# Inverse levels of a recurrent head on half the columns

## The reference

```python
def step(S, inp):
    r_t, w_t, k_t, v_t, a_t, b_t = inp
    Sa = jnp.einsum('bhij,bhj->bhi', S, a_t)
    S = S * w_t[:, :, None, :] + Sa[..., None] * b_t[:, :, None, :] + v_t[..., None] * k_t[:, :, None, :]
    y = jnp.einsum('bhij,bhj->bhi', S, r_t)
    return S, y
...
a = -kk ; b = kk * a_gate        # kk is k, normalised
```

## Time and profile before

| | us |
|---|---|
| median of 3 runs | 897.65 (894.34 to 900.71) |
| the profiled execution | 895.88 |
| its span | 894.1 |
| TensorE matmuls busy | 812.1 (91%) |
| TensorE weight loads busy | 510.3 (57%) |
| Vector engine busy | 457.0 (51%) |
| ScalarE busy | 248.7 (28%) |

### The profile page before, as it was taken

The page is one execution under the profiler, slowest core; times in us unless marked ns, Lnnn a source line. Parts: engine busy times, 40 slices in busy tenths (PEclk is TensorE's granted clock), DMA queues, the critical chain, the costliest instruction groups (busy, mean ns, idle before and its releaser), DMA issues.

```text
span 894.1 us, 16251 instructions
## 1 busy us (share of the span) xinstructions
PE 812.1 (91%) x6152; PEld 510.3 (57%) x6152; DVE 457.0 (51%) x1065; ACT 248.7 (28%) x584; POOL 64.8 (7%) x72
## 2 busy tenths in 40 slices
PE   3999999999999999999999989979899988888780
PEld 3566666666666666666666655456555544445440
DVE  1376687686686786886875936143221111111114
ACT  4123342351441432433423523220111111111112
POOL 1000000000000000000000000000322222222110
PEclk9999999999999999999999999975999999999995
DMA  9252060060250140320600512993999999999955
GB/s 221 78 134 73 25 167 15 25 170 8 58 144 23 45 134 23 105 73 23 166 12 23 165 30 60 375 413 119 344 386 387 385 396 391 392 392 388 399 203 180
DMA packets 114225, 159.85 MB, mean 179 GB/s; under 512 B 27470, under 2 KB 91528, under 8 KB 105974
## 3 DMA queue, kind: packets, MB, share of 16 engines
q1 hardware_dynamic: 98180, 149.14, 48.6%
q0 software_dynamic: 5136, 6.04, 2.5%
q10 hardware_dynamic: 10867, 4.09, 1.9%
HBM read 155.99 MB, written 13.64 MB: 190 GB/s over the span
## 4 chain that ended last, share of the span: by engine, by line
PE 70%; DMA 10%; DVE 8%; SPq 7%; issue 3%; ACT 1%; ACTq 1%; DVEq 0%; POOLq 0%
PE bank L627 17%; PE bank L1008 7%; SPq L457 5%; PE bank L633 4%; PE bank L914 4%; PE bank L795 4%; PE bank L1015 3%; PE bank L858 3%; DMA scratch<-in_exp_up 3%; DMA wall<-in_exp_up 3%; PE bank L738 3%; DMA vecs<-in_exp_up 2%; PE bank L649 2%; PE bank L745 2%; DVE vecs L1465 2%
## 5 line engine op out<-in xcount | busy, mean ns | idle before, releaser
L627 PE MATMUL bank<-xnT,wall 128*128 128x320 f32 x656 | 195.3, 442 | 1.8 <-DVE wkv L1571 1.8
L627 PEld LDWEIGHTS bank<-xnT,wall 128*128 128x128 f32 x656 | 119.0, 190 | 51.5 <-DVE wkv L1571 5.4
L1813 DVE SCALAR_TENSOR_TENSOR vecs<-vecs,bank 128x128 f32<-128x128 f32 x32 | 9.2, 287 | 144.7 <-ACT vecs L1360 144.7
L1008 PE MATMUL bank<-vecs,scratch 128*64 128x256 f32 x448 | 56.5, 409 | 9.1 <-DMA vecs<-in_exp_up 8.2
L1008 PE MATMUL bank<-scratch 128*64 128x256 f32 x384 | 45.8, 393 | 11.8 <-DMA scratch<-in_exp_up 10.6
L1809 DVE COPY vecs<-bank 128x512 f32<-128x512 f32 x32 | 22.1, 691 | 58.1 <-PE bank L1015 42.3
L1008 PEld LDWEIGHTS bank<-vecs,scratch 128*64 128x64 f32 x448 | 33.5, 147 | 28.1 <-DMA vecs<-in_exp_up 9.6
L533 POOL DMA_INDIRECT merged<-xn2d,gidx x4 | 3.7, 918 | 622.5 <-DVE gidx L1791 621.6
L1360 ACT ACTIVATE vecs<-bank 128x128 f32<-128x128 f32 x32 | 8.9, 277 | 136.9 <-PE bank L1008 136.9
L795 PE MATMUL bank<-xnT,wall 128*128 128x320 f32 x128 | 43.9, 455 | 2.5 <-DVE wkv L1611 2.5
L1008 PEld LDWEIGHTS bank<-scratch 128*64 128x64 f32 x384 | 28.2, 141 | 25.9 <-DMA scratch<-in_exp_up 11.8
(11 more groups left out here) (389 smaller groups left out, 1374.1 us busy)
## 6 DMA issues: line engine op xcount, KB each, us to landing
wall<-in_w_in SPq DMA_DIRECT2D x58, 512.0 KB, 5.6
vecs<-in_exp_gate SPq DMA_DIRECT2D x14, 1024.0 KB
vecs<-in_exp_up SPq DMA_DIRECT2D x14, 1024.0 KB
scratch<-in_exp_gate SPq DMA_DIRECT2D x12, 1024.0 KB
scratch<-in_exp_up SPq DMA_DIRECT2D x12, 1024.0 KB
scratch<-in_exp_down SPq DMA_DIRECT2D x7, 1024.0 KB
wall<-in_exp_down SPq DMA_DIRECT2D x7, 1024.0 KB
wall<-in_exp_gate SPq DMA_DIRECT2D x6, 1024.0 KB
```

What stands on the lines that cost most here:

```text
L627: q = mm(tpbank(L, name), wbuf[name][:, k, :], xnT[:, k, :], start=(k == 0), stop=(k == KC - 1))
L1008: q = mm(b[64 * f:64 * f + 64, 0:256], xT[:, k, :], w[:, :, k, 128 * f:128 * f + 128], start=(k == 0), stop=(k == KC - 1))
```

## The change

A level's new entries lie in 32 of 64 columns, and now only these are computed.

- `lower(x, k)` views the 32 columns with `c // m % 2 == 0` of each 64: runs of m = 2^k columns, each followed by a gap of m (runs of 2 at level 1, 4, 8 and 16, and one run of 32 at level 5). `packed(x, k)` views 32 dense columns in the same shape.
- `level_w` on TensorE takes `lower(X)` as the moving operand and writes 32 columns for each chunk; DVE multiplies them with the mask's `lower` columns into W, which is now half as wide.
- `level_x` on TensorE moves the 32 columns of W; DVE adds bank 3 only to X's `lower` columns. The transpose of all of X stays.
- The last product of level 5 has W's 32 columns as the stationary operand and the columns 32 to 63 of Y as the moving one: 32x32 results, on partitions 0 to 31 and 64 to 95.
- In front of the wait for it, DVE copies Y into Yd (two copies, one for each head) behind a wait for `lvY` and with a wait for the copies; the two sums then cover 32 partitions and 32 columns of each of four chunks. `DVE_PER` goes from 55 to 57.

```diff
+        def lower(x, k):
+            return x.rearrange("p u (a s m) -> p u a s m", s=2, m=1 << k)[:, :, :, 0, :]
+
+        def packed(x, k):
+            return x.rearrange("p (u a m) -> p u a m", a=CH >> (k + 1), m=1 << k)
...
-                            q = mm(bank[2][at64(e), 64 * u:64 * u + 64], am[at64(e), u, e, 0, :], X[at64(e), u, :], start=True, stop=True)
+                            q = mm(bank[2][at64(e), 32 * u:32 * u + 32], am[at64(e), u, e, 0, :], lower(X[at64(e), u:u + 1, :], k), start=True, stop=True)
...
-                            q = mm(bank[3][at64(e), 64 * u:64 * u + 64], Y[at64(e), u, :], W[at64(e), u, :], start=True, stop=True)
+                            q = mm(bank[3][at64(e), 32 * u:32 * u + 32], Y[at64(e), u, :], W[at64(e), u, :], start=True, stop=True)
...
-                        q = mm(bank[3][at64(e), 64 * u:64 * u + 64], W[at64(e), u, :], Y[at64(e), u, :], start=True, stop=True)
+                        q = mm(bank[3][64 * e:64 * e + 32, 32 * u:32 * u + 32], W[at64(e), u, :], Y[at64(e), u, 32:64], start=True, stop=True)
...
-                    TT(W[:, 0:n, :], bank[2][:, 0:64 * n].rearrange("p (u c) -> p u c", c=CH),
-                       lev[:, k, None, :].broadcast_to([P, n, CH]), MUL).then_inc(S("lvW"), 1)
+                    m = lower(lev[:, k:k + 1, :], k)
+                    TT(packed(W[:, 0:n, :].rearrange("p u c -> p (u c)"), k), packed(bank[2][:, 0:32 * n], k),
+                       m.broadcast_to([P, n, CH >> (k + 1), 1 << k]), MUL).then_inc(S("lvW"), 1)
...
-                    TT(X[:, 0:n, :], X[:, 0:n, :], bank[3][:, 0:64 * n].rearrange("p (u c) -> p u c", c=CH), ADD).then_inc(S("lvX"), 1)
+                    TT(lower(X[:, 0:n, :], k), lower(X[:, 0:n, :], k), packed(bank[3][:, 0:32 * n], k), ADD).then_inc(S("lvX"), 1)
...
                 step(STT(tgx[:], tgx[:], 1.0, xc[:], ADD, MUL))
-                dve.wait_ge(S("lvB"), i * 5 + 5)
                 if first:
                     dve.wait_ge(S("blank"), 1)
+                dve.wait_ge(S("lvY"), i * 6 + 5)
                 for e in range(2):
-                    q = TT(Yd[at64(e), :, e, :], Y[at64(e), 0:4, :], bank[3][at64(e), 0:256].rearrange("p (u c) -> p u c", c=CH), ADD)
+                    go(CP(Yd[at64(e), :, e, :], Y[at64(e), 0:4, :]))
+                ch.wait()
+                dve.wait_ge(S("lvB"), i * 5 + 5)
+                for e in range(2):
+                    r = slice(64 * e, 64 * e + 32)
+                    q = TT(Yd[r, :, e, 32:64], Y[r, 0:4, 32:64], bank[3][r, 0:128].rearrange("p (u c) -> p u c", c=32), ADD)
                 q.then_inc(S("lvY"), 1)
```

More of the change, by code:

```diff
@@ L154 @@
 DVE_LRU, DVE_TAIL = 4, 5
-DVE_PER = 55
+DVE_PER = 57
 def hawk_rwkv7_moe(nc, a, o):
@@ L238, in hawk_rwkv7_moe @@
         Y, Yd = part(5, CH), part(4, 2, CH)
-        X, W, AK = part(5, CH), part(5, CH), part(5, CH)
+        X, AK = part(5, CH), part(5, CH)
+        W = part(5, CH // 2)
         TM = part(960)
```

## The result

The kernel after takes 886.21 us (median of 10 runs, 884.49 to 893.2) where the kernel before takes 897.63 (10 runs, 894.34 to 901.84). The two medians lie 11.4 us apart. The ratio, taken from all the runs and not from the medians, is 0.9889, with an interval of 0.986 to 0.9918: 1.1% or 10.0 us faster, at least 7.4 and at most 12.6. The prediction was 888.5 us with a range of 884 to 896.

The account below looks back on a forecast made before the run. The prediction took TensorE to bound the recurrent stage, with two recurring waits for the Vector engine. Four terms gave 1.0 us in each of seven turns and 1.2 in the last, 8.3 together: 888.5 us, range 884 to 896.

Parts of the forecast that it names:

- What bounds the kernel: Recurrent stage, eight turns: TensorE is full at full clock, so only its waits or shorter instructions of its own count.
- Term 1: Level 2's masked product and sum on the Vector engine: 160 columns instead of 320 save 0.35 us a middle turn.
- Term 2: End of level 5: sums of 128 instead of 256 columns, copies covered, save 0.28 us a turn, at worst 0.13.
- term 4: Last product of level 5 (L784): 32 stationary columns shorten the weight loads, 0.20 us a turn, bounds 0 and 0.3.
- Term 3: Nine product groups of levels 1 to 5: 32 moving columns instead of 64 gain 0.18 us a turn, bounds 0 and 0.36.
- The reading of L885: Group with 64x64 weights, 16 moving columns takes 0.57 us against 0.61: weight loading sets the pace, halving columns gains almost nothing.
- a fixed cost of some 60 columns: Skill rule for TensorE: a one-column matmul takes as long as one with 60; the prediction said the trace sides with it.
- The step that failed: Middle turn: savings at levels 1, 3 and 4 worth nothing; level 5's masked product counted only in the last turn, 0.15.
- Does it reach the end?: Later part: the transfer queue waits for the last turn's merged result, so the whole later part moves with the turns.
- Gain without effect: Rival in the turns: freed stalls meet another late partner, only shorter groups count, 2 to 3 us, 895 us; chance 0.12.
- The columns set the pace: Rival on TensorE: streaming is the limit, 72 groups lose half their time, some 23 us, near 866 us; chance 0.03.
- Slower by runs: Rival on the Vector engine, levels 1 and 2: short column runs cost extra, deciding at 10 ns, 908 us at 16; chance 0.06.

Follow-up runs that it names:

- the first experiment: The kernel before with only the end of level 5 changed (32 stationary and moving columns, copies ahead, small sums): 62.09 us a turn.
- the third experiment: The kernel after with level 4 alone in the old form (64 columns in both products, masked product and sum): 61.46 us a turn.
- the kernel with both moves: The kernel after with reciprocal behind level 2, copies behind level 5's masked product, last product between g2's halves: 60.78 us a turn; ratio 0.9851, later 0.9868.
- the second experiment: The kernel after with TensorE at full width again, the Vector engine still on 32 of each 64 columns: 61.73 us a turn.

## Why the prediction was right

**What bounds the kernel.** Right. The totals fell by 10.0 us (7.4 to 12.6), and the eight turns by 10.6 in TensorE's starts. The forecast of 8.3 lies inside the interval too, so the totals alone would not have shown that part of the gain was missed.

**Term 1.** 0.35 forecast, 0.32 measured; the operations took 0.325 and 0.321 where I had 0.315. The rest of the stall, forecast as 0.19, is 0.22, and went when the reciprocal was moved.

**Term 2.** 0.28 forecast, 0.28 measured, with copies of 0.29 instead of 0.27 and a cover of 0.06 instead of 0.15 us. The sum held by a small margin. The forecast's cover had term 4's earlier product in it; it did not have the 0.13 us that the block in front of the product lost (last line of the table). Against the end of the Vector engine's operation ahead of the copies (L1606, now L1614) the product starts 227.55 - 227.15 = 0.40 us later before and 221.74 - 221.46 = 0.28 after, and in the first experiment, where that block keeps its length, the sums wait 0.23 us for the bank.

**Term 3.** 0.18 forecast, 0.21 measured. The reading of L885 was right in its size. Its reason was half of the truth: the load does not set the pace alone, it is about as long as the stream of 64 columns. The trace does not side with a fixed cost of some 60 columns either: beside 32 stationary columns, 32 moving ones instead of 64 take the group from 0.56 to 0.37 us.

**Term 4.** 0.20 forecast, 0.24 measured. It needed both operands: the load alone, which the term priced, gains 0.05 (0.61 to 0.56), so the size was right and the working only in part.

**The step that failed** is the sentence behind term 1, that the savings at levels 1, 3 and 4 are worth nothing in a middle turn. For levels 1 and 3 it held. For level 4's sum it did not (0.12 us a turn, the third experiment), and for level 5's masked product, which I counted only in the last turn, neither (0.13, the first three experiments together). Both waits are missing in the list because a wait counts there from the modelled end of the matmul before, and at 0.12 and 0.13 us they were shorter than the 0.27 that it hides. I had said this of the list and then measured two blocks by starts, not all. The two are 0.25 us a turn, 1.8 of the 2.3 us by which the forecast of the turns (8.3) fell short of 10.6; the last turn gave 1.5 instead of 1.2.

**Does it reach the end?** Yes, as far as the totals can tell. *Gain without effect* is out, since the turns' 10.6 us lie inside the interval of the totals. *The columns set the pace* is out by the 0.58 us groups. *Slower by runs* is out by the 325 and 292 ns, which lie on the line of the dense columns. The argument against it was weaker than it read: its 0.87 ns a column is the slope between the very two rows it compares, so L1665 had to fit. With term 1's 1.1 ns a column, 8 columns would take 147 ns and the 174 would leave 3 ns a run, still below the 10 at which the rival wins.

## What to carry to other kernels

Measure every block of a full engine from start to start against an undisturbed block of the same size, before saying where another engine's savings are worth nothing: the list of waits showed nothing of a wait below some 0.27 us here. In these small matmuls halving the moving columns gained next to nothing (0.61 to 0.58 us) until the stationary operand had shrunk too (0.56 to 0.37), so look for a product whose result allows both. Where an engine waits for a second one, look first for work of the second that can stand one step later.

## What the runs showed of the hardware

I had not expected that part of a total's scatter can be located. In one profile of the kernel with both moves the granted clock fell to its half level (1.2 GHz) for some 10 us in the last turn; the profile of the same kernel before that kept 2.4 GHz there. In the 5 us ahead of the fall TensorE sat idle for 0.18 us (for ScalarE) and for 0.34 and 0.73 us (for the Vector engine), but in the profile that kept its clock the same three waits stand there with 0.18, 0.35 and 0.74. A window of the one that fell (busy us and count of each engine, then the granted clock):

```profile
503.00:513.00 10.00, 9.89 (x89) 7.08 (x90) 2.75 (x8) 1.76 (x3) 0.00 (x0) 0.51 0.01 2
```

and its eight records, then those of the one that did not:

```profile
510.31 3.96 PE L634 MATMUL bank<-xnT,wall 128*128 128x320 f32 x8
514.21 0.66 PE L745 MATMUL bank<-wkv,scratch 64*64 64x32 f32 x16
```

```profile
508.26 2.42 PE L634 MATMUL bank<-xnT,wall 128*128 128x320 f32 x8
510.62 0.66 PE L745 MATMUL bank<-wkv,scratch 64*64 64x32 f32 x16
```

The eight take 3.90 us instead of 2.36, and from the last turn's first group (499.01 and 499.98) to the end of the eight the one that fell takes 15.20 us instead of 10.64: 4.6 us more. Why it fell inside the turns in one execution of twelve profiled and not in the others stays open.

The runs of the kernel after near 892 us have a lower mean granted clock as well: 0.954 to 0.956 in the six of seventeen that took 891.17 us or more, 0.960 to 0.966 in the others. Where in the program they lose it no profile shows, since none of the profiled executions is among them.

A second part of the scatter lies ahead of the turns. The same 48 records of one projection (L612, in the second experiment L613) take 37.45 - 24.22 = 13.2 us in the profile of the kernel after, 39.91 - 24.98 = 14.9 in its second profile and 41.55 - 25.36 = 16.2 in the second experiment, and the first turns begin at 73.06, 75.52 and 77.16. The column of the granted clock shows 1.00 in all three, so the cause of the slower pace is not shown.
